# Two attention stages of a three-layer kernel: where the softmax division runs, and the order of TensorE's queue in the second

## Chip, cores and metric

One core of one Trainium2 chip. The metric is the device time of one execution in microseconds; the kernel before has a median of 901.17 us over three runs (900.76 to 901.20). About 0.2% of that, 1.8 us, is what a measurement can tell from no change.

## What is computed

A token sequence of 256 x 1024 goes through an attention layer with two mixers (a sparse one over a latent and one with forget gates, 8 heads each), an MLP, a second attention layer (16 heads, with compressed, selected and window branches mixed by gates), another MLP, a final norm and a differential attention layer. Cut to what the change touches:

```python
# first attention layer, both mixers, two heads at a time
p = masked_softmax(logits, mask)          # exp(s - max) / sum
o = p @ v
# second attention layer, one head at a time, two branches a = selected, window
out = gate[a=0] * o_c + gate[a=1] * (softmax(s_s) @ v_s) + gate[a=2] * (softmax(s_w) @ v_w)
```

The kernel divides the exponentials by their row sums before the product with v. In the second layer it multiplies them by the branch's gate in the same instruction.

## The kernel before

Weights are streamed from HBM in units of 128 x 1024. ScalarE (ACT) rounds a unit to a high part (`act_split`, L473) and VectorE (DVE) forms the low part (`dve_split`, L478), so that TensorE (PE) can multiply in three passes (`mm3`, L358 to L360; L396 where a group goes part by part).

The two attention stages lie between projections. The first runs 8 steps, each with two heads (a = 0, 1); the second 16 steps, each with one head and two branches (a = 0, 1). A step has two token tiles (t = 0, 1), so four blocks of probabilities: 128 x 128 for t = 0 and 128 x 256 for t = 1, in a ring of three buffers (`probs`, `DEEP = 3`). No planner orders the work: each engine has its queue written out by hand, one call per iteration `it`, and semaphores join them.

A step `st` passes through these instructions:
- PE scores (`ab_scores` L1100, `c_scores` L1274). They wait until the peaks of two steps earlier are taken, since they reuse its banks.
- DVE peaks (`masked_peak`, L2073): four fused add-and-min instructions from PSUM into `probs`. They wait for the scores, and for the turn of three steps earlier (the ring).
- ACT exponentials (`exponentials`, L1554): four, with the row sums.
- DVE reciprocal of the four sums (`reciprocals`, L2107), which signals `p_recip`.
- The division (`divide`). DVE does the two blocks of a = 0 right behind the reciprocal and signals `p_divided`; GpSimd (POOL) does the two blocks of a = 1 and signals `p_normed`. In the first attention this is a multiplication by one scalar per row (L773), in the second by two, the inverse sum and the gate (L775). For the very first step of the second attention DVE does all four.
- PE turn (`turn_p`, L1051): three transposes of a = 0 into bank `ptp`, three of a = 1 into `acc`. The first part waits for `p_divided`, the second for `p_normed`, and both for the copies of the step before.
- ACT copies the a = 0 part (`p_first`, L1542), DVE the a = 1 part (`p_second`, L2102).
- PE mix with the values (`o_mix` L1062 every step; `c_mix` L1079 and L1084 every second step), then ACT and DVE split its result into high and low (L1562, L2114).

The queues of one iteration are:
- PE, first attention: turn of step it-3, scores of step it, mix of step it-4.
- PE, second attention: turn of step it-3, scores of step it, and at odd `it` a mix of two steps. At some iterations compressed scores (L1285, L1290), query turns (L432) or a turn of compressed weights (L1299) follow. The first mix also waits for a DVE copy (L2481) of iteration 4.
- DVE: reciprocal and division of step it-2, copy of step it-3, low part of an output (`o_to_low`), peaks of step it (in the first attention the low part comes behind the peaks). At some iterations of the second attention there are softmax pieces of the compressed branch (L2459 to L2475) or low parts of queries (L2354).
- ACT: copy of step it-3, high part of an output, exponentials of step it-1.
- POOL: only the divisions, in the order of the steps, behind one rope at the start of the second attention.

At the end of each attention PE goes on to the output projection (L396).

Of the kernel before, what the change touches and what calls it, by code (L numbers as in the profile page):

```python
# [8 lines left out]
ALU = mybir.AluOpType  # L9
# [6 lines left out]
T = SEQ // P  # L16
# [74 lines left out]
def left(g):  # L91

    return g - min(max(g - G_ABO, 0), 2) - min(max(g - G_CO, 0), 2)
# [114 lines left out]
def program(nc, x, stream, consts_d, cols_d, rows_d, sel_d, out):  # L208
    with ExitStack() as ctx:  # L209
# [24 lines left out]
        ones = sb("ones", [P, P])  # L234
# [13 lines left out]
        st = sb("st", [P, 160])  # L248
# [3 lines left out]
        rs = sb("rs", [P, 64, T])  # L252
# [44 lines left out]
        p_recip, p_normed, p_divided = sem("p_recip"), sem("p_normed"), sem("p_divided")  # L297
# [306 lines left out]
        gate_t = gate.rearrange("p (t b c) -> p t b c", t=T, b=3)  # L604
# [100 lines left out]
        STEPS_AB = A_HEADS // 2 + B_HEADS // 2  # L705
        FOX = B_HEADS // 2
        STEPS_C = C_HEADS
# [50 lines left out]

            return (ptp, acc[2])[a]

        POOL_PARTS = ((1, 0), (1, 1))
        DVE_PARTS = ((0, 0), (0, 1))
        ALL_PARTS = DVE_PARTS + POOL_PARTS

        def divide(eng, st, parts):

            for a, t in parts:
                n = (t + 1) * P
                c0 = t * 2 * P + a * n
                rows = probs[:, st % DEEP, c0:c0 + n]  # L770
                inverse = c_stat(rs, st)[:, a, t:t + 1]
                if st < STEPS_AB:
                    last = eng.tensor_scalar(rows, rows, inverse, None, ALU.mult)  # L773
                else:
                    last = eng.tensor_scalar(rows, rows, inverse, gate_t[:, t, 1 + a, st - STEPS_AB:st - STEPS_AB + 1],  # L775
                                             ALU.mult, ALU.mult)
            return last

        def out_bank(b):
# [23 lines left out]
        def c_stat(tile, st):  # L803

            return tile[:, 2 * st:2 * st + 2, :]
# [40 lines left out]
        def _(pe):  # L846
# [192 lines left out]

            def turn_p(st, a):  # L1040

                if a == 0:
                    pe.wait_ge(p_divided, st + 1)
                elif st < STEPS_AB:
                    pe.wait_ge(p_normed, st + 1)
                elif st > STEPS_AB:
                    pe.wait_ge(p_normed, st)
                pe.wait_ge(s_copied, 2 * st)
                pb = probs[:, st % DEEP, :]
                for k, c0 in enumerate((a * P, 2 * P + a * SEQ, 3 * P + a * SEQ)):  # L1050
                    last = nc.tensor.transpose(turned_bank(a)[:, k * P:(k + 1) * P], pb[:, c0:c0 + P], ident)  # L1051
                last.then_inc(s_turned, 1)
# [176 lines left out]
            for k in range(4):  # L1229
# [3 lines left out]
                for j in range(8):  # L1233
# [3 lines left out]
                    last = mm3(misc[0:CG * N_CMP, kv * P:(kv + 1) * P], xw_h[:, cs], xw_l[:, cs],  # L1237
                               wh[:, u % SPLIT, ws], wl[:, u % SPLIT, ws],
                               uu == 0 and j == 0, uu == 1 and j == 7)
# [26 lines left out]
            def c_scores(n):  # L1266

                st = STEPS_AB + n
                if st >= 2:
                    pe.wait_ge(s_peaked, 2 * (st - 1))  # L1270
                banks = [c_bank(st, t).rearrange("p (a k) -> p a k", a=2) for t in range(T)]
                for t in range(T):
                    for part in range(2):
                        last = mm(banks[t], c_q(n)[:, 0, t * P:(t + 1) * P], c_keys(n % CG, part)[:, :, 0:(t + 1) * P],  # L1274
                                  start=part == 0, stop=part == 1, skip_group_check=True)
                    last.then_inc(s_scored, 1)
# [26 lines left out]
            def c_iter(it):  # L1303

                if it == DEEP:
                    pe.wait_ge(ev_act, left(G_CO))
                    pe.wait_ge(ev_dve, left(G_CO))
                if 0 <= it - DEEP < STEPS_C:
                    turn_p(STEPS_AB + it - DEEP, 0)
                    turn_p(STEPS_AB + it - DEEP, 1)  # L1310
                if it < STEPS_C:
                    c_scores(it)
                if it >= 5 and it % 2 == 1:
                    c_mix((it - 5) // 2)
                if it == 1:
                    pe.wait_ge(dve_prep, 10)
                    compressed_scores(range(0, 8))
                if it == 7:
                    pe.wait_ge(q_lo, 12)
                    compressed_scores(range(8, 16))  # L1320
                if it in (3, 5):
                    z = (it + 1) // 2
                    pe.wait_ge(q_roped, 6)
                    if z == 3:
                        pe.wait_ge(q_lo, 10)
                    pe_turn_z(pe, Z_C + z + 1, c_blocks[2 * z + 2:2 * z + 4], c_q_bank(z))
                if it == 4:
                    turn_compressed(0)
                if it == 11:
                    turn_compressed(1)  # L1330
# [599 lines left out]
        def _(pool):  # L1930
            g = nc.gpsimd
# [42 lines left out]

            for st_ in range(STEPS_AB):
                pool.wait_ge(p_recip, st_ + 1)
                divide(g, st_, POOL_PARTS).then_inc(p_normed, 1)
            mlp_rstd(N_M0, 2)
            residual_rstd(N_A1, 3)

# [4 lines left out]
            for it in range(STEPS_C):  # L1985
                if it == 1:
                    pool.wait_ge(ev_act, left(G_CO))
                    pool.wait_ge(ev_dve, left(G_CO))
                    rope(g, pc_, heads_of(Y[:, :, CQ + GW:CQ + 2 * GW], 8), 8, vaf[:, 512:1024], q_roped)
                if 0 < it < STEPS_C:  # L1990
                    pool.wait_ge(p_recip, STEPS_AB + it + 1)
                    divide(g, STEPS_AB + it, POOL_PARTS).then_inc(p_normed, 1)
            mlp_rstd(N_M1, 4)
            pool.wait_ge(o_mixed, 2 * STEPS_AB + BLOCKS_C)
            g.tensor_tensor(fin2, row[:, R_FIN:R_FIN + D], row[:, R_FIN:R_FIN + D], ALU.mult).then_inc(fin_squared, 1)
# [47 lines left out]
        def _(dve):  # L2043
            v_ = nc.vector
# [56 lines left out]
                copies_free(dve, st)  # L2101
                v_.tensor_copy(c_pt(st, 1), turned_bank(1)[:, 0:KEYS]).then_inc(s_copied, 1)  # L2102

            def reciprocals(st, parts=DVE_PARTS):

                dve.wait_ge(s_exped, 2 * st + 2)
                v_.reciprocal(c_stat(rs, st), c_stat(su, st)).then_inc(p_recip, 1)  # L2107
                dve.wait_ge(p_recip, st + 1)
                divide(v_, st, parts).then_inc(p_divided, 1)

            def o_to_low(b):

# [69 lines left out]
            for cc in range(4):  # L2182
                dve.wait_ge(hi_out, cc + 1)
                for c in range(2):
                    k = 2 * cc + c
                    last = v_.scalar_tensor_tensor(out=xl[:, k, :], in0=opening[cc][:, c * SEQ:(c + 1) * SEQ],
                                                   scalar=col[:, G_ATTN0 + k:G_ATTN0 + k + 1],
                                                   in1=xh[:, k, :].bitcast(F32), op0=ALU.mult, op1=ALU.subtract)
# [43 lines left out]
            for u in range(U_ABO):  # L2232
# [20 lines left out]
                if u == U_QI + 3:  # L2253
# [4 lines left out]
                    for c in range(2):  # L2258
                        last = v_.scalar_tensor_tensor(out=xl[:, KD + c, :], in0=ptp[:, c * SEQ:(c + 1) * SEQ],
                                                       scalar=col[:, G_KVN + c:G_KVN + c + 1],  # L2260
                                                       in1=xh[:, KD + c, :].bitcast(F32), op0=ALU.mult,
                                                       op1=ALU.subtract)
# [72 lines left out]
            for k, (a, b) in enumerate(((R_Q1, R_K1), (R_Q2, R_K2))):  # L2335
                last = v_.tensor_tensor_reduce(pt[:, 0, k * HD:(k + 1) * HD], row[:, a:a + HD], row[:, b:b + HD],
                                               1.0, 0.0, ALU.mult, ALU.add, sml[:, 300 + k:301 + k])
# [145 lines left out]
            for it in range(STEPS_C + DEEP):  # L2483
                if it == 1:
                    evac(dve, G_C + 3, U_CQ2 + 4, 1, Y[:, 1, CQ + GW:CQ + 2 * GW], rr(N_A1), GW)
                if 0 <= it - 2 < STEPS_C:
                    reciprocals(STEPS_AB + it - 2, ALL_PARTS if it == 2 else DVE_PARTS)
                if 0 <= it - DEEP < STEPS_C:
                    p_second(STEPS_AB + it - DEEP)
                if it >= 6 and it % 2 == 0:  # L2490
                    o_to_low(STEPS_AB + (it - 6) // 2)
                if it < STEPS_C:
                    peaks(STEPS_AB + it)
                if it == 0:
                    split(U_CO)
                if it in (STEPS_C, STEPS_C + 1):
                    split(U_CO + 1 + it - STEPS_C)
                if it in (4, 6):
                    q_low(it // 2, Z_C + it // 2 + 1, 4 + it)
                if it == 2:  # L2500
                    compressed_logits(0)
                if it == 3:
                    compressed_weights(0)
                if it == 4:
                    compressed_out(0)
                if it == 8:
                    compressed_logits(1)
                if it == 10:
                    compressed_weights(1)
                if it == 11:  # L2510
                    compressed_out(1)
# [278 lines left out]
```

## Time and profile before

| | |
|---|---|
| median of the runs | 901.17 us |
| the profiled execution's own time | 901.27 us |
| its span | 899.2 us |
| PE busy | 873.3 us, 97% of the span |
| DVE busy | 657.5 us, 73% |
| ACT busy | 509.8 us, 57% |
| POOL busy | 115.0 us, 13% |
| first attention | about 88 to 120 us of the span |
| second attention | about 366 to 429 us |

Times in a timeline row are the start in us from the span's start and the time that the row covers; consecutive instructions of one engine overlap by a tenth or two, since the next is issued before the last has drained. So what an instruction costs its queue is the distance to the next start, and what its consumers wait for is its end. An engine's busy share over a stretch says how full its queue is, not whether the end depends on it.

### The profile page before, as it was taken

The page shows a single profiled execution, that of the slowest core. Times are in us where ns is not written, and L with a number is a line of the kernel's source. Part 1 is how long each engine was busy: PE and PEld are TensorE (multiplying, and loading weights), DVE is VectorE, ACT ScalarE, POOL GpSimd, SP SyncE. Part 2 cuts the span into 40 slices and gives each one's busy share as a digit, 9 for nine tenths or more (in the row PEclk, how much of TensorE's full clock was granted, in tenths as well). Part 3 has the DMA queues.
Part 4 walks back from the last instruction along what each step waited for, and adds up shares of the span by engine and source line. Part 5 has one row for each costly group of instructions (what it writes and reads, how often), then busy time and mean ns, then how long its engine had stood idle before and what let it go on. Part 6 is the DMA issues. An engine that isn't in the chain of part 4 may idle for free. (4 is left out here: it accounts for less than half of the span.)

```text
span 899.2 us, 14587 instructions
## 1 busy us (share of the span) xinstructions
PE 873.3 (97%) x4652; PEld 718.8 (80%) x4652; DVE 657.5 (73%) x1372; ACT 509.8 (57%) x1026; POOL 115.0 (13%) x158
## 2 busy tenths in 40 slices
PE   7999999999999999888999999999999999999998
PEld 6778677888888888766878888888887778878876
DVE  4769966666666689899576666666976878877785
ACT  5655845444444465676454444444666666566573
POOL 1310500000000000223010000000520401400401
PEclk9999999999999999999999999999999999999999
DMA  9643053655555547101436555555364444443431
GB/s 335 223 157 127 16 187 136 209 193 191 190 198 191 190 163 253 52 1 47 165 132 220 188 197 194 193 186 188 142 209 141 149 147 174 157 171 141 168 113 47
DMA packets 41607, 145.72 MB, mean 162 GB/s; under 512 B 4688, under 2 KB 6224, under 8 KB 41552
## 3 DMA queue, kind: packets, MB, share of 16 engines
q1 hardware_dynamic: 41264, 144.93, 46.2%
q8 instruction: 33, 0.54, 0.2%
q14 instruction: 22, 0.18, 0.1%
q10 hardware_dynamic: 288, 0.07, 0.0%
HBM read 143.93 MB, written 1.05 MB: 161 GB/s over the span
## 5 line engine op out<-in xcount | busy, mean ns | idle before, releaser
L478 DVE TENSOR_TENSOR wl<-raw,wh 128x1024 fp32r<-128x1024 f32 (+2 forms) x270 | 329.2, 1223 | 90.9 <-ACT wh L473 88.2
L473 ACT ACTIVATE wh<-raw 128x1024 fp32r<-128x1024 f32 (+2 forms) x270 | 281.6, 1046 | 66.2 <-PE acc L360 49.8
L358 PE MATMUL acc<-wh,xhl 128*128 128x512 f32 (+1 forms) x472 | 190.7, 404 | 1.3 <-DVE wl L478 0.9
L360 PE MATMUL acc<-wh,xhl 128*128 128x512 f32 (+1 forms) x472 | 184.4, 391 | 0.0
L359 PE MATMUL acc<-wl,xhl 128*128 128x512 f32 (+1 forms) x472 | 183.9, 390 | 0.0
L358 PEld LDWEIGHTS acc<-wh,xhl 128*128 128x128 f32 x472 | 88.7, 188 | 25.9 <-issue 8.0
L360 PEld LDWEIGHTS acc<-wh,xhl 128*128 128x128 f32 x472 | 88.6, 188 | 19.2
L359 PEld LDWEIGHTS acc<-wl,xhl 128*128 128x128 f32 x472 | 88.8, 188 | 16.3
L358 PE MATMUL acc<-wh,hh 128*128 128x512 f32 x256 | 100.2, 391 | 0.0
L359 PE MATMUL acc<-wl,hh 128*128 128x512 f32 x256 | 100.0, 391 | 0.0
L360 PE MATMUL acc<-wh,hl 128*128 128x512 f32 x256 | 99.6, 389 | 0.0
L1584 ACT ACTIVATE hh<-hq 128x256 fp32r<-128x256 f32 x64 | 26.7, 418 | 77.3 <-PE acc L360 72.5
L1578 ACT ACTIVATE probs<-ptp 128x256 f32<-128x256 f32 x32 | 12.3, 383 | 93.7 <-PE ptp L894 93.7
L887 PE MATMUL ptp<-xhl,wh 128*128 128x512 f32 x256 | 64.1, 390 | 1.1 <-DVE hr L2136 1.1
L887 PE MATMUL misc<-xhl,wh 128*128 128x512 f32 x256 | 64.3, 391 | 0.6 <-DVE hr L2136 0.6
L2136 DVE TENSOR_TENSOR hr<-ptp,probs 128x256 f32<-128x256 f32 x32 | 13.6, 424 | 67.5 <-ACT probs L1578 67.5
L522 POOL TENSOR_SCALAR st<-st 128x2 f32<-128x2 f32 x7 | 2.4, 338 | 430.7 <-ACT o_tok L515 258.1
L887 PEld LDWEIGHTS misc<-xhl,wh 128*128 128x128 f32 x256 | 47.7, 188 | 11.2 <-DVE wl L478 1.5
L887 PEld LDWEIGHTS ptp<-xhl,wh 128*128 128x128 f32 x256 | 47.8, 188 | 11.2 <-issue 1.4
L360 PEld LDWEIGHTS acc<-wh,hl 128*128 128x128 f32 x256 | 48.1, 188 | 10.2
L358 PEld LDWEIGHTS acc<-wh,hh 128*128 128x128 f32 x256 | 48.2, 188 | 9.2
L359 PEld LDWEIGHTS acc<-wl,hh 128*128 128x128 f32 x256 | 48.2, 188 | 8.7
(322 smaller groups left out, 1306.0 us busy)
## 6 DMA issues: line engine op xcount, KB each, us to landing
raw<-stream SPq DMA_DIRECT2D x266, 512.0 KB, 3.3
raw<-stream SPq DMA_DIRECT2D x4, 352.0 KB, 6.7
h<-x SPq DMA_DIRECT2D x4, 256.0 KB, 4.0
out<-h SPq DMA_DIRECT2D x3, 256.0 KB, 2.1
row<-rows SPq DMA_DIRECT2D x1, 700.0 KB, 9.6
probs<-sel SPq DMA_DIRECT2D x1, 512.0 KB, 8.3
cst<-consts SPq DMA_DIRECT2D x1, 507.0 KB, 7.7
out<-h SPq DMA_DIRECT2D x2, 128.0 KB, 2.0
```

What stands on the lines that cost most here:

```text
L358: nc.tensor.matmul(out_, ah, bh, start=start, stop=False, skip_group_check=True)
L359: nc.tensor.matmul(out_, ah, bl, start=False, stop=False, skip_group_check=True)
L360: return nc.tensor.matmul(out_, al, bh, start=False, stop=stop_, skip_group_check=True)
L473: nc.scalar.activation(used(u, wh[:, u % SPLIT, :]), used(u, raw[:, u % RAW, :]), ACT.Copy).then_inc(w_hi, 1)
L478: nc.vector.tensor_tensor(used(u, wl[:, u % SPLIT, :]), used(u, raw[:, u % RAW, :]), used(u, wh[:, u % SPLIT, :]).bitcast(F32), ALU.subtra ...
L522: chain_link(nc.gpsimd.tensor_scalar(dst, src, 1.0 / width, EPS, ALU.mult, ALU.add))
L887: nc.tensor.matmul((ptp, misc)[f % 2][:, :], wh[:, u % SPLIT, k * P:(k + 1) * P], xhl[:, KD + k, :, :].rearrange("p a s -> p (a s)"), star ...
L1578: s_.activation(probs[:, f % 2, 0:SEQ], (ptp, misc)[f % 2][:, SEQ:2 * SEQ], ACT.Copy).then_inc(z_cross, 1)
L1584: s_.activation(hh[:, f % 2, :], hq[:, f % 2, :], ACT.Copy).then_inc(hid_hi, 1)
L2136: v_.tensor_tensor(hr[:, f % 2, :], bank[:, 0:SEQ], probs[:, f % 2, 0:SEQ], ALU.add).then_inc(z_summed, 1)
```

## The change

In both attentions all four blocks of a step are divided on GpSimd, a = 0 first, with a signal behind each a. Every such instruction has two scalars: in the first attention the second one is a column of ones. DVE keeps the division of the first step of the second attention, all four blocks. PE's two turns of a step wait for the first and the second signal. In the second attention PE's queue has the scores of step it ahead of the turn of step it-3.

```diff
-        def divide(eng, st, parts):
-            for a, t in parts:
+        def divide(eng, st, a):
+            for t in range(T):
                 n = (t + 1) * P
                 c0 = t * 2 * P + a * n
                 rows = probs[:, st % DEEP, c0:c0 + n]
-                inverse = c_stat(rs, st)[:, a, t:t + 1]
                 if st < STEPS_AB:
-                    last = eng.tensor_scalar(rows, rows, inverse, None, ALU.mult)
+                    factor = ones[:, 0:1]
                 else:
-                    last = eng.tensor_scalar(rows, rows, inverse, gate_t[:, t, 1 + a, ...], ALU.mult, ALU.mult)
+                    factor = gate_t[:, t, 1 + a, ...]
+                last = eng.tensor_scalar(rows, rows, c_stat(rs, st)[:, a, t:t + 1], factor, ALU.mult, ALU.mult)
             return last
...
             def turn_p(st, a):
-                if a == 0:
-                    pe.wait_ge(p_divided, st + 1)
-                elif st < STEPS_AB:
-                    pe.wait_ge(p_normed, st + 1)
-                elif st > STEPS_AB:
-                    pe.wait_ge(p_normed, st)
+                if st == STEPS_AB:
+                    pe.wait_ge(p_divided, 1)
+                else:
+                    pe.wait_ge(p_normed, 2 * (st - (st > STEPS_AB)) + a + 1)
                 pe.wait_ge(s_copied, 2 * st)
...
             def c_iter(it):
+                if it < STEPS_C:
+                    c_scores(it)
                 if 0 <= it - DEEP < STEPS_C:
                     turn_p(STEPS_AB + it - DEEP, 0)
                     turn_p(STEPS_AB + it - DEEP, 1)
-                if it < STEPS_C:
-                    c_scores(it)
...
             # gpsimd, both attentions
-                divide(g, st_, POOL_PARTS).then_inc(p_normed, 1)
+                for a in range(2):
+                    divide(g, st_, a).then_inc(p_normed, 1)
...
             def reciprocals(st):
                 dve.wait_ge(s_exped, 2 * st + 2)
                 v_.reciprocal(c_stat(rs, st), c_stat(su, st)).then_inc(p_recip, 1)
-                dve.wait_ge(p_recip, st + 1)
-                divide(v_, st, parts).then_inc(p_divided, 1)
+                if st == STEPS_AB:
+                    dve.wait_ge(p_recip, st + 1)
+                    divide(v_, st, 0)
+                    divide(v_, st, 1).then_inc(p_divided, 1)
```

## Rows read from the trace of the kernel before

**Rows 1.** Busy time of each engine by stretch: the two attentions (PE, PEld, DVE, ACT, POOL, clock).
```profile
85.00:117.00 32.00, 29.98 (x220) 21.20 (x219) 28.92 (x122) 23.84 (x85) 13.16 (x16) 1.00 0.15 51
...
364.00:430.00 66.00, 56.12 (x389) 42.78 (x388) 59.51 (x236) 45.46 (x164) 18.84 (x36) 0.97 0.10 33
```

**Rows 2.** Timeline of DVE, first attention: one step, and a later reciprocal.
```profile
103.09 0.17 DVE L2107 RECIPROCAL rs<-su 128x4 f32<-128x4 f32 x1
103.29 0.66 DVE L773 TENSOR_SCALAR probs<-probs,rs 128x128 f32<-128x128 f32 x2
103.87 0.54 DVE L2102 COPY pt<-acc 128x384 f32<-128x384 f32 x1
104.34 0.28 DVE L2073 CUSTOM_DVE_ANT_0 probs<-pair,picked 128x128 f32<-128x128 f32 x1
...
105.78 0.16 DVE L2107 RECIPROCAL rs<-su 128x4 f32<-128x4 f32 x1
...
108.47 0.16 DVE L2107 RECIPROCAL rs<-su 128x4 f32<-128x4 f32 x1
```

**Rows 3.** Timeline of PE, first attention: turn, scores, mix, next turn.
```profile
102.23 0.55 PE L1051 MATMUL ptp<-cst,probs 128*128 128x128 f32 x3
...
103.03 0.37 PE L1100 MATMUL pair<-QK 64*128 64x128 f32 x1
...
103.89 0.87 PE L1062 MATMUL misc<-pt,Y 128*64 128x256 f32 x8
104.69 0.55 PE L1051 MATMUL ptp<-cst,probs 128*128 128x128 f32 x3
```

**Rows 4.** Timeline of DVE, second attention: two steps between reciprocals.
```profile
408.68 0.17 DVE L2107 RECIPROCAL rs<-su 128x4 f32<-128x4 f32 x1
...
411.64 0.73 DVE L775 TENSOR_SCALAR probs<-probs,rs,sml 128x128 f32<-128x128 f32 x2
412.29 0.54 DVE L2102 COPY o_tok<-acc 128x384 f32<-128x384 f32 x1
...
413.85 0.17 DVE L2107 RECIPROCAL rs<-su 128x4 f32<-128x4 f32 x1
```

**Rows 5.** Timeline of PE, second attention: turn and scores, mix, next turn.
```profile
410.22 0.52 PE L1051 MATMUL ptp<-cst,probs 128*128 128x128 f32 x3 [1.20 <-DVE pt L2102]
...
411.69 1.52 PE L1079 MATMUL misc<-pt,Y 128*64 128x256 f32 x16
...
413.68 0.49 PE L1051 MATMUL ptp<-cst,probs 128*128 128x128 f32 x3
```

**Rows 6.** Groups by shape of POOL's divisions, one scalar, first attention.
```profile
L773 POOL TENSOR_SCALAR probs<-probs,rs 128x256 f32<-128x256 f32 x8 | 7.3, 917 | 0.0
L773 POOL TENSOR_SCALAR probs<-probs,rs 128x128 f32<-128x128 f32 x8 | 6.0, 744 | 50.4 <-DVE rs L2107 50.4
```

**Rows 7.** Groups by shape of POOL's divisions, two scalars, second attention.
```profile
L775 POOL TENSOR_SCALAR probs<-probs,rs,sml 128x256 f32<-128x256 f32 x15 | 8.7, 578 | 0.0
L775 POOL TENSOR_SCALAR probs<-probs,rs,sml 128x128 f32<-128x128 f32 x15 | 7.8, 518 | 33.8 <-DVE rs L2107 33.8
```

**Rows 8.** Timeline, first attention: a POOL division, then the PE turn behind it.
```profile
106.04 1.65 POOL L773 TENSOR_SCALAR probs<-probs,rs 128x128 f32<-128x128 f32 x2 [1.04 <-DVE rs L2107]
...
107.74 0.55 PE L1051 MATMUL acc<-cst,probs 128*128 128x128 f32 x3
```

**Rows 9.** Timeline: where PE enters the first output projection.
```profile
111.71 1.20 PE L396 MATMUL acc<-wh,xhl 128*128 128x512 f32 x4
```

**Rows 10.** Timeline: last reciprocal of the second attention, and PE's output projection.
```profile
421.96 0.17 DVE L2107 RECIPROCAL rs<-su 128x4 f32<-128x4 f32 x1
...
424.10 1.17 PE L396 MATMUL acc<-wh,xhl 128*128 128x512 f32 x4
```

**Rows 11.** Timeline: first mix of the second attention, and the next turn.
```profile
384.68 1.52 PE L1079 MATMUL misc<-pt,Y 128*64 128x256 f32 x16 [1.45 <-DVE hr L2481]
...
387.11 0.49 PE L1051 MATMUL ptp<-cst,probs 128*128 128x128 f32 x3
```

More of the change, by code:

```diff
@@ L759, in turned_bank @@
             return (ptp, acc[2])[a]
-        POOL_PARTS = ((1, 0), (1, 1))
-        DVE_PARTS = ((0, 0), (0, 1))
-        ALL_PARTS = DVE_PARTS + POOL_PARTS
-        def divide(eng, st, parts):
-            for a, t in parts:
+        def divide(eng, st, a):
+            for t in range(T):
                 n = (t + 1) * P
@@ L770, in divide @@
                 rows = probs[:, st % DEEP, c0:c0 + n]
-                inverse = c_stat(rs, st)[:, a, t:t + 1]
                 if st < STEPS_AB:
-                    last = eng.tensor_scalar(rows, rows, inverse, None, ALU.mult)
+                    factor = ones[:, 0:1]
                 else:
-                    last = eng.tensor_scalar(rows, rows, inverse, gate_t[:, t, 1 + a, st - STEPS_AB:st - STEPS_AB + 1],
-                                             ALU.mult, ALU.mult)
+                    factor = gate_t[:, t, 1 + a, st - STEPS_AB:st - STEPS_AB + 1]
+                last = eng.tensor_scalar(rows, rows, c_stat(rs, st)[:, a, t:t + 1], factor, ALU.mult, ALU.mult)
             return last
@@ L1991, in _ @@
                     pool.wait_ge(p_recip, STEPS_AB + it + 1)
-                    divide(g, STEPS_AB + it, POOL_PARTS).then_inc(p_normed, 1)
+                    for a in range(2):
+                        divide(g, STEPS_AB + it, a).then_inc(p_normed, 1)
             mlp_rstd(N_M1, 4)
@@ L2102, in p_second, with reciprocals @@
                 v_.tensor_copy(c_pt(st, 1), turned_bank(1)[:, 0:KEYS]).then_inc(s_copied, 1)
-            def reciprocals(st, parts=DVE_PARTS):
+            def reciprocals(st):
                 dve.wait_ge(s_exped, 2 * st + 2)
                 v_.reciprocal(c_stat(rs, st), c_stat(su, st)).then_inc(p_recip, 1)
-                dve.wait_ge(p_recip, st + 1)
-                divide(v_, st, parts).then_inc(p_divided, 1)
+                if st == STEPS_AB:
+                    dve.wait_ge(p_recip, st + 1)
+                    divide(v_, st, 0)
+                    divide(v_, st, 1).then_inc(p_divided, 1)
             def o_to_low(b):
@@ L2486, in _ @@
                 if 0 <= it - 2 < STEPS_C:
-                    reciprocals(STEPS_AB + it - 2, ALL_PARTS if it == 2 else DVE_PARTS)
+                    reciprocals(STEPS_AB + it - 2)
                 if 0 <= it - DEEP < STEPS_C:
```

## The prediction

> **What bounds the kernel now.** I read the busy time of the two attentions first, then DVE's and PE's timelines there, then POOL's divisions by shape. A change in these stages is worth what it moves PE's entry into the output projection, since from there PE runs without a gap again.
>
> DVE is the fullest queue whose time is all real work: 28.92 of 32 us in the first attention and 59.51 of 66 in the second [rows 1]. Its timeline shows why: reciprocal follows reciprocal after 2.69 us in the first attention (103.09, 105.78, 108.47), and after 5.17 us per two steps, 2.59 each, in the second [rows 2, 4]. There is no idle row between. The divisions hold 0.58 us of each step (103.29 to 103.87) and 0.65 us (411.64 to 412.29).
>
> PE looks like the loser who waits for DVE, and is nearly as full. In the first attention one step is turn 0.80 (102.23 to 103.03), scores 0.86 (to 103.89), mix 0.80 (to 104.69): 2.46 us [rows 3]. In the second, turn and scores together are 1.47 (410.22 to 411.69) and a mix 1.99 (to 413.68), so two steps are 2 x 1.47 + 1.99 = 4.93 us, 2.47 each [rows 5]. So behind DVE's 2.69 and 2.59 stands a floor at 2.46 and 2.47. Taking 0.6 us a step from DVE can't give more than 0.23 and 0.12 us a step where a step has nothing extra.
>
> **What is removed.** From DVE 8 x 0.58 = 4.6 us and, as the very first step of the second attention stays, 15 x 0.65 = 9.75 us: 14.4 us of queue.
>
> **What is added.** POOL does four blocks where it did two. With two scalars a pair costs 0.518 + 0.578 = 1.10 us, four blocks 2.19 [rows 7]; with one scalar, as now in the first attention, a pair costs 0.744 + 0.917 = 1.66 [rows 6]. The column of ones makes the first attention's instruction the one of rows 7, so I take 2.19 for both; 3.32 stays as the other end. As a throughput 2.19 is under every period above. As a latency it counts: from a reciprocal's start, 0.17 until it ends, 0.10 until POOL starts (DVE ends at 105.94, POOL starts at 106.04), then POOL; 0.26 is taken for the two together. PE's second turn starts 0.05 us behind POOL's end (107.69 to 107.74) [rows 2, 8]. So a = 0 is ready after 0.26 + 1.10 + 0.05 = 1.41 us, where DVE's part was ready after about 1.1 (0.20 + 0.66, and some 0.15 to PE), and a = 1 after 0.26 + 2.19 + 0.05 = 2.50, where it was 1.97 in the first attention and 1.41 in the second.
>
> **The loop that this makes, first attention.** PE's order is not changed there. Second turn at R + 2.50, then 0.42 of queue, scores readable 0.92 later (turn at 102.23, scores at 103.03, first peak after it as DVE allows; estimate), 0.05 to DVE, then peaks and low part 1.44 (104.34 to 105.78) [rows 2, 3]. The reciprocal behind these peaks is that of two steps later: 2.50 + 0.42 + 0.97 + 1.44 = 5.33, 2.67 a step against 2.69. Without a low part, in the early steps, it is 5.00 per two steps, where DVE now needs 2 x (2.69 - 0.33) = 4.72. So the first attention wins 0.29 at its start (half a division in front of the first peaks), loses 0.26 in the early steps and holds its pace after. At its end PE leaves 2.50 + 0.42 + 0.81 = 3.73 us behind the reciprocal of the last but one step, where it is now 111.71 - 108.47 = 3.24 [rows 2, 9]. Sum: -0.29 + 0.26 + 0.03 + 0.49 = **+0.5 us**.
>
> **Second attention.** Here the scores stand ahead of the turn, so DVE's peaks don't wait for them: 2.50, turn's end 0.54 later, copy 0.47, peaks 1.11, and every other step 0.33 of low part, 4.62 or 4.95 per two steps. PE needs 4.93. Both are just under today's 5.17. I stepped the four queues through the 16 steps in their new order, each instruction starting when its predecessor's slot (distances as above) and its releaser's end allow; the same stepping of the old order puts reciprocals of plain steps within 0.6 us of the trace and PE's exit at 423.65 against 424.10 [rows 10], so I use differences alone. The new order is ahead by 1.95 us at the fifth step, since each of these steps lost 0.65 us of a full DVE. Then the first mix, which waits for a DVE copy of iteration 4 and starts at 384.68 now [rows 11], holds PE, and behind it 0.87 us of scores now stand ahead of the turn that ACT, and behind ACT everything, is waiting for: the lead falls to 0.4. It grows again to 1.96 by the thirteenth step, in the steps in which DVE has softmax pieces of the compressed branch besides, falls to 1.1 as PE's 4.93 and its scores ahead of the turns take over, and at the exit PE leaves 2.50 + 0.25 = 2.75 us behind the last reciprocal, where it is 424.10 - 421.96 = 2.14 now [rows 10]: 0.6 more. What is left is **-0.5 us**.
>
> Moving the scores is by itself worth nothing or a loss: where PE waits for the division it fills the wait, where PE is the late one it puts 0.87 us ahead of the turn. No bound in the rows excludes a loss of 0.9 from it, nor a gain of as much where the peaks waited for scores.
>
> Sum: 0.5 - 0.5 = 0. Against the profiled execution's 901.27, which stands 0.1 above the median, this is 901.2 us for the median.
>
> [...] POOL's pair takes 1.10 us where DVE's slot for the same two blocks is 0.65, a factor of 1.7 [rows 4, 7]. [...]
>
> **Rivals.**
> - *DVE's time is paid out* (faster, 22%). Where DVE has extra pieces, in about five steps of the second attention, its 0.65 us is the whole step's gain, and if PE fills its waits with the moved scores, these 3.3 us are kept: 897.9. For it: DVE is full in rows 1 and waits for nobody. Against: the two-step loop and PE's 4.93 stand right behind.
> - *POOL becomes the bound of the first attention* (slower, 8%). If its time there is not a matter of the number of scalars but of the place, four blocks take 3.32 us, over the 2.67 of the loop; each of 8 steps is then 3.4 instead of 2.69, +5 us: 906.3. It decides from about 2.3 us for four blocks on. Rows 6 and 7 have the same shapes in both places, which speaks for the number of scalars.
> - *POOL is held while DVE splits weights* (slower, 10%). At the ends of the attentions a 1.2 us DVE split now falls into POOL's four blocks. If POOL stands still for it, the last turn of the second attention is 1.2 us later and the loop loses some 1 us more in all: 903.3. Now POOL's blocks and splits hardly meet, so no row decides. [...]
> - *The time only changes its holder* is my forecast itself (60%): DVE's queue gets its 14.4 us of room and PE leaves both attentions when it did.
>
> **Chances and range.** Within 1.8 us of 901.2 lies the forecast, 60%. Faster by more than that 22%, by the first rival. Slower 18%, by the other two. The range runs from 898.4, where most of the first rival is taken in, to 903.3, the price of the held POOL; the 906 case is left out. The forecast's own range is 900 to 902.5, from the uncertainty of the latencies: each 0.1 us on the way from POOL to PE costs 0.5 us in the second attention and 0.1 in the first.
>
> **What would show it.** POOL's divisions in the first attention should be 0.52 and 0.58 us. DVE should show idle time where it has none, ending with PE's turn of a = 1 or ACT's exponentials. Reciprocals in the first attention should stay 2.6 to 2.7 apart, PE should enter the first output projection 0.3 to 0.8 us later (measured against its own start), and leave the second attention 0 to 1 us earlier relative to its start. Turns should follow POOL's end by 0.05 us. I am wrong if PE has waits left in the second attention that were counted as work, or if the granted clock of PE falls to its lower level in a stretch in which it is full now.

## The result, and the profile after

The changed kernel takes 903.78 us (median of 20 runs, 901.64 to 906.09), the kernel before 901.0 (20 runs, 900.53 to 901.44): a ratio of 1.0032, 95% interval 1.0026 to 1.0038. I forecast 901.2 within 898.4 to 903.3. It is slower by 2.8 us, where I had said no change, and it has a spread of 4.5 us where the kernel before has 0.9.

The profiled execution has a span of 902.2 us against 899.2. First the groups by shape of POOL's divisions, which answer to [rows 6, 7] (the count, then busy us and mean ns of one, then idle us before and what ended it):

```profile
L771 POOL TENSOR_SCALAR probs<-probs,rs,sml 128x256 f32<-128x256 f32 x30 | 17.6, 587 | 0.0
L771 POOL TENSOR_SCALAR probs<-probs,rs,sml 128x128 f32<-128x128 f32 x30 | 13.4, 447 | 19.3 <-DVE rs L2102 19.2
L771 POOL TENSOR_SCALAR probs<-probs,rs,ones 128x256 f32<-128x256 f32 x16 | 8.8, 553 | 0.0
L771 POOL TENSOR_SCALAR probs<-probs,rs,ones 128x128 f32<-128x128 f32 x16 | 8.1, 507 | 47.5 <-DVE rs L2102 47.5
```

The column of ones does what it says: the first attention's blocks went from 744 and 917 ns to about those of the second. But a mean hides something. The source view of the same line gives minimum, median and maximum:

```profile
L771 POOL TENSOR_SCALAR probs<-probs,rs,sml x60: 440/500/1516, 377.1 to 422.6; 128x128 f32<-128x128 f32 x30, 128x256 f32<-128x256 f32 x30
L771 POOL TENSOR_SCALAR probs<-probs,rs,ones x32: 440/547/1409, 90.9 to 112.4; 128x128 f32<-128x128 f32 x16, 128x256 f32<-128x256 f32 x16
```

A block that takes about 0.55 us (0.45 for 128 x 128) took 1.5 once in the second attention and 1.4 in the first. The timelines of POOL, DVE and PE at the end of the second attention show where:

```profile
419.73 1.52 POOL L771 TENSOR_SCALAR probs<-probs,rs,sml 128x256 f32<-128x256 f32 x1
```
```profile
419.60 1.22 DVE L478 TENSOR_TENSOR wl<-raw,wh 128x1024 fp32r<-128x1024 f32 x1
420.74 0.17 DVE L2102 RECIPROCAL rs<-su 128x4 f32<-128x4 f32 x1
...
422.71 1.53 DVE L478 TENSOR_TENSOR wl<-raw,wh 128x1024 fp32r<-128x1024 f32 x1
```
```profile
421.30 0.90 PE L1044 MATMUL acc<-cst,probs 128*128 128x128 f32 x3 [1.28 <-POOL probs L771]
...
422.13 2.83 PE L1072 MATMUL misc<-pt,Y 128*64 128x256 f32 x16
424.89 1.22 PE L1077 MATMUL misc<-hr,ka 128*128 128x256 f32 x2
425.90 0.85 PE L1044 MATMUL ptp<-cst,probs 128*128 128x128 f32 x3
...
427.04 1.23 PE L396 MATMUL acc<-wh,xhl 128*128 128x512 f32 x4
```

Read together: DVE's weight split runs from 419.60 to 420.82, and the POOL block that starts at 419.73 ends at 421.25, just behind it. PE waits 1.28 us for it. At the next meeting the roles are turned: POOL is at work (its block of 422.62 takes its usual 0.55 us), and DVE's split takes 1.53 us instead of 1.22. And then PE itself is slow. Its mix takes 3.77 us (422.13 to 425.90) where it took 1.99 [rows 5], the last turn 1.14 (425.90 to 427.04) where it took 0.60 (423.50 to 424.10 in the kernel before). The busy time by stretch (PE, PEld, DVE, ACT, POOL, granted clock, DMA share, GB/s) says why:

```profile
418.00:420.00 2.00, 1.05 (x6) 0.62 (x6) 1.38 (x4) 2.00 (x10) 1.82 (x5) 1.00 0.00 0
420.00:422.00 2.00, 0.72 (x4) 0.50 (x3) 0.91 (x2) 0.79 (x3) 2.00 (x3) 0.58 0.03 10
422.00:424.00 2.00, 2.00 (x13) 1.31 (x14) 1.76 (x2) 0.00 (x0) 1.17 (x3) 0.50 0.71 252
424.00:426.00 2.00, 2.00 (x11) 1.20 (x8) 0.24 (x1) 0.00 (x0) 0.00 (x0) 0.50 0.29 57
426.00:428.00 2.00, 2.00 (x11) 1.87 (x10) 0.62 (x2) 1.21 (x3) 0.00 (x0) 0.71 0.51 205
```

In shorter stretches the fall itself can be seen:

```profile
420.00:420.25 0.25, 0.02 (x1) 0.00 (x0) 0.25 (x1) 0.25 (x2) 0.25 (x1) 1.00 0.00 0
420.25:420.50 0.25, 0.00 (x0) 0.00 (x0) 0.25 (x1) 0.25 (x3) 0.25 (x1) 0.68 0.00 0
420.50:420.75 0.25, 0.00 (x0) 0.00 (x0) 0.25 (x2) 0.25 (x1) 0.25 (x1) 0.50 0.00 0
```

PE was busy 1.05 us of the 2 us up to 420 and then idle until 421.30. Its granted clock falls within this wait, between 420.25 and 420.50, from 1.00 to 0.50, and stays there until after 426.75: through the second part of the turn, the mix and the last turn, which lead to the exit. In the kernel before PE is as full there (2.00 of 2 us from 422 to 426), at a granted clock of 1.00.

**Where the 3 us are.** I measure each stage against its own start. First attention, PE's first turn to its output projection: 112.36 - 93.17 = 19.19 us, against 111.71 - 93.72 = 17.99: +1.2. Second attention, first scores (366.61, was 366.03) to the last reciprocal: 54.13 against 55.93: -1.8. From there to PE's exit: 6.30 against 2.14 [rows 10]: +4.2. The sum is 3.6; the first turn comes 0.55 earlier in the span than before, which leaves the 3.0 of the spans. So the division's move won in the middle of the second attention what it was meant to win, and more than that was lost in its last 6 us.

The stretch view of the kernel before has a like dip of the clock early in the second attention (0.89, 0.50 and 0.76 in the three stretches from 372 to 378 us); the changed kernel has it too (0.84, 0.50 and 0.80 from 378 to 384). It is in both, of the same size, and explains no difference between these two traces.

In the first attention the same meeting stands at the end: DVE's split starts at 108.75 and POOL's block of 109.08 takes 1.41 us. PE's timeline:

```profile
111.08 0.55 PE L1044 MATMUL acc<-cst,probs 128*128 128x128 f32 x3 [1.38 <-POOL probs L771]
...
112.36 1.20 PE L396 MATMUL acc<-wh,xhl 128*128 128x512 f32 x4
```

Here PE waits 1.38 us, and in this trace its clock stays at 1.00.

### The profile page after: what moved, and what is told of

It is laid out like the page before. It is cut to its first block and busy times, and to the rows that moved or that the text cites. A ratio compares the mean times of both kernels' runs of the same rounds, so it can differ in the third digit from the quotient of the medians.

```text
span 902.2 us, 14588 instructions
## 1 busy us (share of the span) xinstructions
PE 878.4 (97%) x4652; PEld 721.6 (80%) x4652; DVE 643.8 (71%) x1326; ACT 509.3 (56%) x1026; POOL 132.1 (15%) x204
## 3 DMA queue, kind: packets, MB, share of 16 engines
HBM read 143.93 MB, written 1.05 MB: 161 GB/s over the span
```

## Experiments

Theory 1: DVE's weight splits, which stand near the end of both attentions, hold POOL now that POOL works twice as long on every step; PE stands idle for it, and its clock falls. Theory 2: POOL's plain latency is too long. Theory 3: the scores ahead of the turns cost the time. Every kernel below is compared with the kernel before, run beside it on the same chip; the ratios are to that (901.07 us for late_splits, fill_pe, old_order and order_only, 901.16 for late_old, before_late, one_scalar and best, 901.17 for late_c, late_ab and mid_splits). Differences from the changed kernel's 903.78, or from a kernel of another group, go across chips, on which the kernel before differs by 0.2 at most.

**late_splits.** The two splits at each end are moved to where POOL is done or has slack.

```diff
-                if it in (STEPS_AB, STEPS_AB + 1):
-                    split(U_ABO + 1 + it - STEPS_AB)
+                if it in (STEPS_AB + 1, STEPS_AB + 2):
+                    split(U_ABO + it - STEPS_AB)
...
-                if it in (STEPS_C, STEPS_C + 1):
-                    split(U_CO + 1 + it - STEPS_C)
+                if it == STEPS_C + DEEP - 1:
+                    split(U_CO + 1)
+                    split(U_CO + 2)
```

> The changed kernel with DVE's two weight splits at the end of each attention moved behind POOL's last long work (second attention: both behind the last copy; first attention: one iteration later each). Theory 1 (POOL is held while DVE splits, PE then stands idle and its clock falls): the 1.2 us hold before the last turns goes, PE keeps full clock at the end of the second attention, exit at most 2.9 us behind the last reciprocal where the changed kernel has 6.3; time 899.5 to 901 and little spread between runs. Theory 2 (POOL's plain latency of 2.2 us for four blocks is too long in any case): at most 1 us is recovered, 903. Theory 3 (the scores ahead of the turns do it): nothing changes, 903.8.

900.83 us (899.30 to 901.93), ratio 0.9996 (0.9988 to 1.0005): 2.95 us of the changed kernel's time go with the place of four instructions. The source view of POOL's line, the stretches and PE's exit of this kernel:

```profile
L771 POOL TENSOR_SCALAR probs<-probs,rs,sml x60: 447/503/563, 376.2 to 421.2; 128x128 f32<-128x128 f32 x30, 128x256 f32<-128x256 f32 x30
```
```profile
416.00:418.00 2.00, 1.38 (x8) 0.62 (x6) 1.06 (x8) 2.00 (x10) 1.82 (x5) 1.00 0.02 4
418.00:420.00 2.00, 1.14 (x8) 0.76 (x10) 0.94 (x4) 1.83 (x9) 1.56 (x4) 1.00 0.00 0
420.00:422.00 2.00, 2.00 (x20) 1.44 (x19) 0.52 (x1) 0.00 (x0) 1.71 (x4) 1.00 0.00 0
```
```profile
419.49 0.18 DVE L2102 RECIPROCAL rs<-su 128x4 f32<-128x4 f32 x1 [0.77 <-ACT probs L1547]
...
422.42 1.17 PE L396 MATMUL acc<-wh,xhl 128*128 128x512 f32 x4
```

The longest block of the second attention is 563 ns, the clock stays at 1.00, and the exit is 2.93 us behind the last reciprocal instead of 6.30. Theory 1 holds, and its 2.9 was met; the spread, 2.6 us, stayed larger than the "little" that I expected. The first attention takes 111.35 - 93.12 = 18.23 us, so of its 1.2 us only 0.24 is left for POOL's latency. POOL is still held once there, as the same view of the first attention's blocks shows:

```profile
L771 POOL TENSOR_SCALAR probs<-probs,rs,ones x32: 447/502/1520, 90.8 to 111.7; 128x128 f32<-128x128 f32 x16, 128x256 f32<-128x256 f32 x16
```

But the held block (111.73) now belongs to the last step, whose turn stands behind PE's entry into the projection (114.21). So it is the place of the hold that counts, not that there is one.

**late_c, late_ab.** Each half of that edit alone.

> The changed kernel with only the second attention's two weight splits moved behind its last copy. If that attention's end (POOL held, then the clock) is where most of the loss is: 3.0 us less a part for the first attention, 901.3 to 902; the first attention as in the changed kernel, PE's exit 19.2 us behind its first turn. If the two attentions share the loss evenly: 902.3.

> The changed kernel with only the first attention's two weight splits one iteration later. Together with late_c this should make up late_splits' 3.0 us: 0.9 us of it here, 902.9, with the clock at the end of the second attention still falling and the spread between runs still some 4 us.

902.12 us (901.59 to 903.69), ratio 1.0011 (1.0002 to 1.0019), and 903.32 (900.61 to 903.88), ratio 1.0015 (1.0005 to 1.0025). The second attention's end is worth 1.7 us of the 3.0, the first's 0.5: less than I expected for both, and they don't quite add up (2.1). With medians of kernels whose runs differ by 2 to 3 us that is no finding by itself, but the traces show a part of it. late_c's exit is 424.72 - 421.80 = 2.92 us behind its last reciprocal, as in late_splits. But the clock falls a second time in the middle of the stage, in a stretch for which the changed kernel's trace has 1.00:

```profile
394.00:396.00 2.00, 2.00 (x9) 1.70 (x9) 0.00 (x0) 0.00 (x0) 2.00 (x5) 0.50 0.00 0
```

Its stage up to the last reciprocal takes 421.80 - 366.70 = 55.10 us, against 54.13 in the changed kernel and 419.49 - 365.68 = 53.81 in late_splits. Why the clock falls there in one execution and not in another stays open.

late_ab's trace holds something that I hadn't expected. It keeps the splits at the end of the second attention, POOL's block of 420.96 takes 1.52 us, and PE waits exactly as long as in the changed kernel, but at a granted clock of 1.00 all the way:

```profile
421.98 0.17 DVE L2102 RECIPROCAL rs<-su 128x4 f32<-128x4 f32 x1
```
```profile
422.54 0.55 PE L1044 MATMUL acc<-cst,probs 128*128 128x128 f32 x3 [1.28 <-POOL probs L771]
423.01 1.52 PE L1072 MATMUL misc<-pt,Y 128*64 128x256 f32 x16
...
425.75 1.17 PE L396 MATMUL acc<-wh,xhl 128*128 128x512 f32 x4
```

The exit is 3.77 us behind the last reciprocal. That separates the two costs: 3.77 - 2.93 = 0.84 us for the held POOL, and 6.30 - 3.77 = 2.53 us for the clock. It also shows that the clock needn't fall in this wait: PE's three parts of turns start at 418.21, 419.50 and 421.30 in the changed kernel and at 419.45, 420.74 and 422.54 in late_ab, each 1.24 us later, so PE did the same in the 3 us ahead of its end.

**fill_pe.** Does the clock cost time, or does it only go along with the wait? PE gets products of a zero tile while it waits for the held POOL.

```diff
+                    if it == STEPS_C + 1:
+                        keep_clock(acc[3], 4)
                     turn_p(STEPS_AB + it - DEEP, 0)
+                    if it == STEPS_C + 1:
+                        keep_clock(acc[3], 6)
                     turn_p(STEPS_AB + it - DEEP, 1)
```

> The changed kernel with ten products of a zero tile (nothing of the output depends on them, 2.1 us at full clock) put into PE's queue ahead of the two parts of the turn of the second attention's last step but one, where PE waits for POOL. If the loss is in part the clock that falls behind this wait: granted clock 0.998 in every run, spread between runs below 1 us, time 901 to 902.3, with POOL held as long as ever. If the clock only falls for what came before or costs nothing: 904 to 906, the fill added.

901.71 us (901.34 to 903.26), ratio 1.0008 (1.0 to 1.0017). The stretches of this kernel, and its mix:

```profile
418.00:420.00 2.00, 1.58 (x11) 1.04 (x9) 1.06 (x5) 2.00 (x9) 1.82 (x5) 1.00 0.02 4
420.00:422.00 2.00, 2.00 (x12) 1.50 (x12) 1.35 (x3) 1.24 (x5) 2.00 (x3) 1.00 0.00 0
422.00:424.00 2.00, 2.00 (x21) 1.34 (x20) 1.67 (x2) 0.00 (x0) 2.00 (x4) 1.00 0.79 250
```
```profile
422.22 1.52 PE L1072 MATMUL misc<-pt,Y 128*64 128x256 f32 x16
423.67 0.70 PE L1077 MATMUL misc<-hr,ka 128*128 128x256 f32 x2
```

The ten products hold PE's queue from 418.95 to 419.97 and from 420.22 to 421.75, 1.02 + 1.53 = 2.55 us, where I had 2.1. This work, which computes nothing, made the kernel 2.1 us faster. The clock stays at 1.00, the mix is back at 1.99 us (422.22 to 424.21), and the spread shrinks from 4.5 to 1.9 us. The split still runs at 420.04, and PE leaves 3.75 us (424.94 - 421.19) behind the last reciprocal: 0.8 more than with late splits, which is the held POOL without the clock, as in late_ab. Nine of eleven runs had a clock of 0.998, two 0.996 (both at 903.3); I had expected all eleven, and a spread below 1.

The changed kernel's 20 runs go the same way: at a mean granted clock of 0.998 two runs of 901.6 and 901.9 us, at 0.996 six from 902.7 to 903.4, at 0.994 and 0.992 twelve from 903.5 to 906.1. So without the clock the change costs an estimated 0.8 us (901.6 and 901.9 against 901.0, two runs only); the rest goes with a clock that falls or doesn't. A run's mean clock doesn't say where it fell. That it fell at the exit is seen in the one run that was traced, and fill_pe, which changes nothing but the exit, makes it likely for most of the others.

**old_order.** PE's scores behind the turns again, all else as changed.

```diff
-                if it < STEPS_C:
-                    c_scores(it)
                 if 0 <= it - DEEP < STEPS_C:
                     turn_p(STEPS_AB + it - DEEP, 0)
                     turn_p(STEPS_AB + it - DEEP, 1)
+                if it < STEPS_C:
+                    c_scores(it)
```

> The changed kernel with PE's scores behind the two turns again, as before; all divisions stay on GpSimd. Theory 3 (the order costs): back to about 901. Theory 1: the last two turns have no scores ahead of them in either order, so POOL is held as before there and the clock falls; 903 to 904, perhaps 0.9 less by what the order costs in the middle.

902.14 us (900.17 to 903.63), ratio 1.0012 (1.0003 to 1.002): 1.6 of the 2.8 us. More than the 0.9 that I gave the order, less than theory 3 needs. Its trace, a run of 903.37, shows POOL held (a block of 1525 ns) and a granted clock of 0.50 at the exit, from 423 to 426 us, as theory 1 wants.

**order_only.** The same order put into the kernel before.

> The kernel before with only PE's scores ahead of the turns in the second attention; divisions shared as before. By the stepping behind the prediction plus 0.9 us: 901.9. Theory 3 wants plus 2.8. Theory 1 wants between 0 and 0.9, with the clock as in the kernel before.

902.24 us (901.22 to 904.19), ratio 1.0019 (1.001 to 1.0028): +1.2. Its runs fall into two bunches, six at clock 0.998 from 901.2 to 902.2 and five at 0.994 from 903.2 to 904.2. The first bunch, 0.8 above the kernel before, is the order's own price: its traced run takes 422.36 - 365.50 = 56.86 us from the first scores to the last reciprocal, against 55.93, and the same 2.14 to the exit. The second bunch goes with a lower mean clock; no trace shows where it fell.

**late_old.** Both repairs in the changed kernel.

> The changed kernel with both repairs: the weight splits late, as in late_splits, and PE's scores behind the turns, as before. If the held POOL and the order are separate costs, this is late_splits less what the order costs in the middle (0.9 by the stepping, 1.2 by order_only): 899.7 to 900, 1.2 us below the kernel before. If the order only mattered together with the held POOL (late scores and the clock), it is late_splits again, 900.8.

898.78 us (897.91 to 899.38), ratio 0.9974 (0.9962 to 0.9985), 2.4 us under the kernel before and 2.0 under late_splits: the order costs without the held POOL too, and more than I thought. Its first scores, last reciprocal and exit are at 365.50, 418.40 and 420.98: 52.90 us to the reciprocal (was 55.93) and 2.58 from there (was 2.14). Its reciprocals show where the order costs. From the fifth to the sixth it takes 390.06 - 384.12 = 5.94 us, in late_splits 390.95 - 384.30 = 6.65; from the seventh to the eighth 396.63 - 391.86 = 4.77, against 398.25 - 392.74 = 5.51. PE is full in the first of these stretches (1.97 to 2.00 of every 2 us from 384 to 390 in late_splits) and has its scores (385.11 to 385.90) ahead of the turn for which DVE waits 2.28 us. This is the fastest version here, with best.

**before_late.** The control: late splits with shared divisions.

> Control: the kernel before with its weight splits moved as in late_splits, divisions shared. DVE's splits hardly meet POOL there. If late_splits won by freeing POOL, this is the kernel before within 0.7 us (901.1), by DVE's queue at most 0.6 better. If the splits' place matters by itself (a DVE queue less full at the end), it wins the 3 us that late_splits won over the changed kernel: 898 to 899.

901.0 us (900.5 to 901.64), ratio 0.9996 (0.9987 to 1.0005). The splits' place is worth nothing where they don't keep PE's next turn from its blocks.

**one_scalar.** The changed kernel without the column of ones.

```diff
-                last = eng.tensor_scalar(rows, rows, c_stat(rs, st)[:, a, t:t + 1], factor, ALU.mult, ALU.mult)
+                inverse = c_stat(rs, st)[:, a, t:t + 1]
+                if st < STEPS_AB:
+                    last = eng.tensor_scalar(rows, rows, inverse, None, ALU.mult)
+                else:
+                    last = eng.tensor_scalar(rows, rows, inverse, factor, ALU.mult, ALU.mult)
```

> The changed kernel with one scalar per division in the first attention instead of the inverse and a column of ones. If the number of scalars sets POOL's 744 and 917 ns, four blocks are 3.3 us there, POOL is the bound of that stage, and the time is 5 us above the changed kernel: 908 to 909.5. If the place or its neighbours set it, 903.8.

909.37 us (908.09 to 910.51, four runs), ratio 1.0093 (1.0077 to 1.011), 5.6 above the changed kernel. POOL's groups by shape in it:

```profile
L773 POOL TENSOR_SCALAR probs<-probs,rs 128x256 f32<-128x256 f32 x16 | 14.9, 932 | 0.0
...
L773 POOL TENSOR_SCALAR probs<-probs,rs 128x128 f32<-128x128 f32 x16 | 11.5, 717 | 43.8 <-DVE rs L2106 43.7
```

These means hide held blocks again (the longest takes 1669 ns). From 95.5 to 105 us, where no split runs, they are

```profile
L773 POOL TENSOR_SCALAR probs<-probs,rs 128x256 f32<-128x256 f32 x6 | 5.5, 922 | 0.0
L773 POOL TENSOR_SCALAR probs<-probs,rs 128x128 f32<-128x128 f32 x6 | 3.6, 602 | 1.3 <-DVE rs L2106 1.3
```

On the same data in the same place a multiplication by one scalar takes 1.52 us a pair, one by two scalars 1.00 (447 and 554 ns in the changed kernel, over the same stretch). Four blocks are then 3.05 us, not the 3.3 that I expected: of the 744 ns of [rows 6], some 140 weren't the scalar's but came with DVE's division beside it. Still POOL is the bound: the first attention takes 116.47 - 93.74 = 22.73 us.

**best.** The name was too early. First attention shared as before, but with two scalars on both engines, and with its splits in their old place; second attention as in late_old.

```diff
             def reciprocals(st):
...
+                if st < STEPS_AB:
+                    dve.wait_ge(p_recip, st + 1)
+                    divide(v_, st, 0).then_inc(p_divided, 1)
                 if st == STEPS_AB:
```

> A version that takes from each: in the first attention DVE divides a = 0 and POOL a = 1 as before, but with two scalars; in the second all on POOL, the scores behind the turns and the splits behind the last copy. The first attention should be that of the kernel before or 0.1 to 0.2 better, and so 0.2 to 0.4 better than late_old's; 899.4 to 899.8. If all of POOL's work in the first attention costs nothing once its splits are late, the same as late_old.

898.98 us (898.15 to 900.5), ratio 0.9978 (0.9967 to 0.9989): not apart from late_old's 898.78. Who divides in the first attention is worth nothing, as long as no hold falls on PE's way out: from the first turn to the projection it takes 111.30 - 93.08 = 18.22 us, late_old 18.23. I had expected the 17.99 of the kernel before or less. DVE's pair takes 0.73 us with two scalars where it took 0.66 with one [rows 2], and its reciprocals are 2.75 apart instead of 2.69.

**mid_splits.** The second attention's splits in the middle of the stage.

```diff
-                if it in (STEPS_C, STEPS_C + 1):
-                    split(U_CO + 1 + it - STEPS_C)
+                if it in (10, 12):
+                    split(U_CO + 1 + (it - 10) // 2)
```

> The changed kernel with the second attention's two weight splits in DVE's iterations 10 and 12, right behind peaks, in the middle of the stage. They hold POOL there as long (a 128x128 or 128x256 block of 1.4 to 1.5 us). If a hold costs wherever it falls, since POOL is on the two-step loop: 1 to 2 us more than late_c for the two, but without the clock's fall at the end, 902.5 to 903.5. If a hold costs only at the end, where no other step covers it: as late_c within 0.5 us.

903.77 us (903.16 to 905.5, five runs), ratio 1.0034 (1.0021 to 1.0047), 1.65 above late_c. The number is in the expected place, the reason isn't. The source view of POOL's line in it:

```profile
L771 POOL TENSOR_SCALAR probs<-probs,rs,sml x60: 451/509/568, 377.2 to 425.4; 128x128 f32<-128x128 f32 x30, 128x256 f32<-128x256 f32 x30
```

No block was held: the splits (405.38 and 412.80) fell where POOL had nothing to do. They cost as DVE's own time: the reciprocal behind the first comes 408.01 - 402.24 = 5.77 us after the one before it, in late_c 4.62, and behind the second it is 413.93 - 409.99 = 3.94 against 2.79. So whether a hold in mid-stage would cost something stays untested.

## Why the prediction was wrong

The step that failed is "the time only changes its holder", and in it a term of the sum on the second attention, that PE leaves 2.75 us behind the last reciprocal. It left 6.30 behind it; 2.93 where nothing held POOL (late_splits). Two things were missing in the sum.

**POOL held by a DVE split.** I had it as a rival with one chance in ten and a price of 2.2 us in all. The meeting was not a matter of chance: DVE's queue puts a split into two of the second attention's last three iterations, beside POOL's work on a step, and every trace here with the splits in that place and all divisions on POOL has a held block, of 1.51 to 1.53 us (after, fill_pe, old_order, late_ab, one_scalar). What I left open was only whether POOL stands still for it. Its own price is about 0.8 to 1 us at each end (3.77 - 2.93 = 0.84 in the second attention, 19.19 - 18.23 = 0.96 in the first), 1.8 in all. So the price was about right and the chance was wrong. I wrote that no row decides; the trace of the changed kernel does, with 1.52 us for a block of 0.55. What it is in a split that holds POOL, its two inputs from SBUF, its form or its length, isn't shown: no run varies them. DVE's low part of an output, which has one of its two inputs in PSUM and takes 0.41 us, runs at 419.27 in the changed kernel beside a POOL block of 419.30, and that takes its usual 447 ns.

**The clock.** I named it as the thing that would make me wrong and gave it no price, and so it went: it was at 0.50 from 420.3 to 427, and from 422 on PE is full in the kernel before. At half the clock the products on the way to the exit take up to twice as long: 0.41 us more for the second part of the turn (0.83, was 0.42), 1.78 for the mix and 0.54 for the last turn, 2.7 in all, and 2.53 by the exits of late_ab and the changed kernel. Without the fallen clock the change would stand at about 901.8 by the estimate above, inside my range, with POOL held and the middle of the stage better than I had it, which would have been luck in part. The other 2 us, and most of the spread, are the clock's, as far as fill_pe and the mean clocks tell.

Point by point:
- *DVE's queue gets room.* Right. Busy time in the second attention's window (364 to 430 us) went from 59.51 [rows 1] to 48.62 us.
- *POOL with ones costs 2.19 for four blocks.* Right in kind (one_scalar), too dear in size: undisturbed it is 2 x (0.447 + 0.555) = 2.00 us. The 518 and 578 ns of [rows 7] were taken with DVE's own divisions beside them, which are gone; best has them back in the first attention, and its blocks take 522 and 582 ns again.
- *First attention +0.5.* Measured +1.2, and +0.24 with the splits out of the way. The loop's pace was about right on average: the last four distances between reciprocals add up to 110.11 - 99.82 = 10.29 us, 2.57 each, though singly from 2.26 to 2.77. Its latency was 0.2 too long: PE leaves 111.35 - 107.80 = 3.55 us behind the last reciprocal but one in late_splits, where I had 3.73, and 4.51 with POOL held.
- *Second attention -0.5.* Up to the last reciprocal I had -1.1, measured -1.8. The stepping was too careful by 0.7, perhaps by POOL's time; that isn't shown. In the old order without held POOL the stage gives 58.07 - 55.48 = 2.6 us.
- *Moving the scores is worth nothing or a loss, of up to 0.9.* Right in sign: 0.8 without the clock, 1.2 in medians, 1.6 and 2.0 in the changed kernels. I took it too cheap there. The stepping had the place: the steps behind the first mix.
- *The rival "POOL becomes the bound of the first attention", +5 us.* The price was about right (5.6 in one_scalar); the condition didn't hold.
- *The rival "DVE's time is paid out", 897.9.* Not for this change, but late_old has 898.78: the division's move gains, and the change as it stands loses it through the place of the splits and the order of the scores.

## What to carry to other kernels

Before work moves to GpSimd, look which DVE instructions stand beside it in the queues, above all near a stage's end; here a weight split of 1.22 us made a GpSimd block of 0.55 us take 1.52, and the place of four splits decided between 903.8 and 900.8 us. A wait of TensorE ahead of a dense stretch can cost more by the clock that falls in it than by its own length: here a wait of 1.28 us cost 0.8 us in one traced execution, with a granted clock of 1.00, and 2.5 us more in another, with 0.50. So when a kernel's runs spread more than before, look at the granted clock of each run, and at the trace for where it fell. When PE's order is changed to fill a wait, ask first in which iterations PE is the late one: there the filler stands in front of what everybody waits for.

## What was not expected of the hardware

- A GpSimd multiplication by one scalar per row is slower than one by two: 602 and 922 ns against 447 and 554 for 128 x 128 and 128 x 256 in the same place, and 5.6 us of the kernel's time hang on it.
- GpSimd's 128 x 128 block with two scalars takes 448 ns in the first attention of late_old (up to 105 us, where no split runs) and 522 in that of best, where DVE divides beside it; with one scalar it is 602 (one_scalar) and 744 [rows 6]. So DVE's division goes with a slower GpSimd, by some 75 and 140 ns; no other neighbour of DVE's was tried.
- The hold goes both ways: a DVE split that starts while GpSimd works took 1.53 us instead of 1.22. But not every meeting costs: in the kernel before, a split starts at 110.05, in the last 0.33 us of a block of 128 x 256 with one scalar, and neither is longer than elsewhere (1.21 us and 918 ns).
- The same wait of 1.28 us for the same held block left PE at a granted clock of 0.50 in one traced execution (the changed kernel's) and of 1.00 in another (late_ab's).
- Ten products of a zero tile, 2.55 us of PE's queue, took 2.1 us off the kernel.
